# Sample states as the moving operand in a hybrid decoder step: four 32-column tiles, a predicated copy and two fold products

## What is computed

```python
def hgrn2_chunk(S, q, k, v, logf):
    b = jnp.cumsum(logf, axis=1)
    ...
    o = jnp.einsum('bhts,bshv->bthv', att, v) + jnp.einsum('bthk,bhkv->bthv', q * jnp.exp(b), S)
    b_last = b[:, -1]
    k_dec = k * jnp.exp(b_last[:, None] - b)
    S_new = jnp.exp(b_last)[..., None] * S + jnp.einsum('bshk,bshv->bhkv', k_dec, v)
    return S_new, o
```

## Time and profile before

| What | Value |
|---|---|
| Median of 3 runs | 1325.11 us (1325.05 to 1325.72) |
| The profiled execution, its own time | 1324.93 us |
| Its span, first to last instruction | 1323.0 us |
| TensorE, matmul / weight load busy | 1286.8 / 1224.3 us |
| VectorE / ScalarE / GpSimd busy | 585.6 / 519.6 / 261.1 us |
| Stage of the eight heads, within the span | about 61 to 550 us |

### The profile page before, as it was taken

How to read it: one execution, slowest core, us unless ns; L and a number is a source line. 1 busy time by engine, 2 the same in 40 slices (tenths; PEclk the granted TensorE clock), 3 DMA queues, 4 the chain that set the end, 5 groups by cost and what they waited for, 6 DMA issues and landing times.

```text
span 1323.0 us, 22284 instructions
## 1 busy us (share of the span) xinstructions
PE 1286.8 (97%) x8892; PEld 1224.3 (93%) x8892; DVE 585.6 (44%) x1213; ACT 519.6 (39%) x1035; POOL 261.1 (20%) x119
## 2 busy tenths in 40 slices
PE   4999999999999999999999999999999999999998
PEld 4999999999999999999999999999998899999885
DVE  5546657574847465600000155555555202335122
ACT  6453635445353535511111255555555314114111
POOL 0222221222322222222222111111110111342000
PEclk9999999999999999999999999999999899999999
DMA  6212121302021221121111311111100312241330
GB/s 197 66 33 66 35 64 34 79 18 79 18 79 34 78 56 43 34 64 48 48 41 43 84 33 33 33 33 33 33 17 1 106 32 64 58 102 33 116 126 37
DMA packets 136767, 73.85 MB, mean 56 GB/s; under 512 B 37185, under 2 KB 133138, under 8 KB 136690
## 3 DMA queue, kind: packets, MB, share of 16 engines
q1 hardware_dynamic: 136706, 72.99, 20.0%
HBM read 63.77 MB, written 10.22 MB: 56 GB/s over the span
## 4 chain that ended last, share of the span: by engine, by line
PE 62%; issue 25%; POOL 6%; DVE 4%; ACT 2%; DMA 1%; SPq 0%; POOLq 0%; ACTq 0%
PE pj L972 43%; POOL w_l L560 5%; PE pj L988 3%; PE pj L1319 3%; DVE scores L1595 2%; PE ps_a L1319 1%; PE ps_e L1319 1%; PE ps_e L1210 1%; PE ps_a L1175 1%; PE ps_d L1210 1%; DVE scores L1583 1%; PE ps_d L1319 1%; PE ps_b L1319 1%; PE ps_c L1319 1%; PE ps_a L1198 1%
## 5 line engine op out<-in xcount | busy, mean ns | idle before, releaser
L972 PE MATMUL pj<-xn_h,w_h 128*128 128x352 f32 x1704 | 563.2, 330 | 5.6 <-POOL w_l L560 2.1
L972 PE MATMUL pj<-xn_h,w_l 128*128 128x352 f32 x1704 | 551.5, 324 | 0.0
L972 PE MATMUL pj<-xn_l,w_h 128*128 128x352 f32 x1704 | 551.2, 323 | 0.0
L560 POOL TENSOR_TENSOR w_l<-w_raw,w_h 128x1024 fp32r<-128x1024 f32 x82 | 203.4, 2480 | 689.8 <-ACT w_h L632 689.8
L972 PEld LDWEIGHTS pj<-xn_h,w_h 128*128 128x128 f32 x1704 | 323.7, 190 | 15.1 <-issue 5.3
L972 PEld LDWEIGHTS pj<-xn_l,w_h 128*128 128x128 f32 x1704 | 324.4, 190 | 0.1
L972 PEld LDWEIGHTS pj<-xn_h,w_l 128*128 128x128 f32 x1704 | 323.8, 190 | 0.0
L632 ACT ACTIVATE w_h<-w_raw 128x1024 fp32r<-128x1024 f32 x82 | 86.4, 1054 | 114.4 <-PE pj L972 100.2
L1552 DVE TENSOR_TENSOR mg<-sg,pj 128x352 f32 (+1 forms) x24 | 12.4, 522 | 151.8 <-PE pj L972 150.4
L840 ACT ACTIVATE scores<-scores,stat 128x256 f32<-128x256 f32 (+1 forms) x128 | 61.4, 481 | 0.0
L972 PE MATMUL pj<-hl_l,w_h 128*128 128x352 f32 x168 | 54.2, 323 | 0.0
(11 more groups left out here) (361 smaller groups left out, 2014.4 us busy)
## 6 DMA issues: line engine op xcount, KB each, us to landing
w_raw<-in_w_in_dram SPq DMA_DIRECT2D x132, 256.0 KB, 3.4
x_t<-in_x_prompt_dram SPq DMA_DIRECT2D x8, 512.0 KB, 9.4
s<-in_state_hgrn_dram SPq DMA_DIRECT2D x8, 512.0 KB, 4.2
out_dram<-s SPq DMA_DIRECT2D x8, 512.0 KB, 3.2
w_raw<-in_w_pa_dram SPq DMA_DIRECT2D x16, 256.0 KB, 3.0
w_raw<-in_w_pb_dram SPq DMA_DIRECT2D x16, 256.0 KB, 4.3
wo_raw<-in_w_out_dram SPq DMA_DIRECT2D x8, 512.0 KB, 3.6
x_o<-in_x_prompt_dram SPq DMA_DIRECT2D x8, 512.0 KB, 4.1
```

Of the source, the lines that this page charges most:

```text
L560: g.tensor_tensor(w_l[p][:], w_raw[p][:], w_h[p][:].bitcast(F32), ALU.subtract).then_inc(w_lo_ready, 1)
L972: mm = nc.tensor.matmul(pj[g][:, 0:W], w[:, kt, :], x[:, kt, span(g)], start=(kt == 0 and m == 0), stop=(kt == KT - 1 and m == 2))
```

## The change

The sample part of `os` is taken apart. A new step `cr` on TensorE, behind `ps` and ahead of `u0`, takes the queries of all 32 sample tokens (`qI[:, SEQ:T]`, 128x32) as the stationary operand and streams each of the 8 states (128 columns) past them, into one of four groups of 32 partitions of `ps_e`, two states side by side. So every token's query meets every state. VectorE then copies, by a predicate `own`, only those rows in which token and state belong together, into an SBUF tile `cross` of 128x256 that is otherwise zero (step `crm`, ahead of `att0`). Last, `os` becomes three products of 32 moving columns: the one with `att_s` as before and two with the halves of `cross` as the stationary operand and a constant `fold` (128x32, a sum of identity columns) as the moving one. `fold`, the zeros in `cross` and `own` are made once ahead of the heads, `own` from four small loads. The wait for `s0` and the one for `qI` on TensorE move up to `cr`, and `s8` waits for `cr` in place of `ps`, since both lie in `ps_e`. GpSimd's program is the same.

```diff
-    masked = ["att0", "att1", "atts"]
+    masked = ["crm", "att0", "att1", "atts"]
...
+        cross = sb("cross", [P, 2, P])
+        fold = sb("fold", [P, NS])
+        own_b = sb("own_b", [P, NB])
+        own = sb("own", [P, 2])
...
+            for j in range(4):
+                sp.dma_start(own_b[j * NS:(j + 1) * NS, :], c_batch[0:NS, :]).then_inc(own_loaded, 16)
...
                 nc.tensor.matmul(ps_e[0:NS, 256:256 + NS], dk[:, SEQ:T], dq[:, SEQ:T], start=True, stop=True).then_inc(pe_done, pe.tick(now, "ps"))
+
+                t.wait_ge(s0_loaded, i * 16 + 16)
+                t.wait_ge(dve_done, dve.at(now, "qIm"))
+                for m in range(NB):
+                    j = m % 4
+                    mm = nc.tensor.matmul(ps_e[j * NS:(j + 1) * NS, m // 4 * P:(m // 4 + 1) * P], qI[:, SEQ:T], s0[:, m, :], start=True, stop=True)
+                mm.then_inc(pe_done, pe.tick(now, "cr"))
...
                 t.wait_ge(dve_done, dve.at(now, "atts"))
-                t.wait_ge(dve_done, dve.at(now, "qIm"))
...
-                t.wait_ge(s0_loaded, i * 16 + 16)
-                nc.tensor.matmul(ps_d[:, 0:NS], v_tok[0:NS, NC, :], att_s[:, :], start=True, stop=True)
-                for m in range(NB):
-                    e = SEQ + DEC * m
-                    mm = nc.tensor.matmul(ps_d[:, DEC * m:DEC * (m + 1)], s0[:, m, :], qI[:, e:e + DEC], start=False, stop=True, skip_group_check=True)
-                mm.then_inc(pe_done, pe.tick(now, "os"))
+                nc.tensor.matmul(ps_d[:, 0:NS], v_tok[0:NS, NC, :], att_s[:, :], start=True, stop=False)
+                nc.tensor.matmul(ps_d[:, 0:NS], cross[:, 0, :], fold[:], start=False, stop=False)
+                nc.tensor.matmul(ps_d[:, 0:NS], cross[:, 1, :], fold[:], start=False, stop=True).then_inc(pe_done, pe.tick(now, "os"))
...
+            v.tensor_reduce(fold[:], ident[:].rearrange("p (j t) -> p t j", j=4), mybir.AxisListType.X, ALU.add).then_inc(dve_done, dve.tick(pr, "fold"))
+            v.memset(cross[:], 0.0).then_inc(dve_done, dve.tick(pr, "cross0"))
+            v.wait_ge(own_loaded, 64)
+            for j in range(4):
+                rows_j = slice(j * NS, (j + 1) * NS)
+                v.tensor_copy(own[rows_j, :], own_b[rows_j, j::4]).then_inc(dve_done, dve.tick(pr, f"own{j}"))
...
-                        need(pe, pe_done, "ps")
+                        need(pe, pe_done, "cr")
...
+                v.copy_predicated(cross[:], own[:].bitcast(I32).rearrange("p (h o) -> p h o", o=1).to_broadcast([P, 2, P]),
+                                  ps_e[:, 0:2 * P].rearrange("p (h v) -> p h v", h=2)).then_inc(dve_done, done("crm"))
```

More of the change, by code:

```diff
@@ L144, in hybrid_step @@
         ("pro", ["par", "lbm", "lbd0", "lbd1", "lbs", "lbr", "lb", "oml", "noml", "mean"] + per_tile(["xn"], ["lo_a", "lo_b"])
-         + ["att0", "atts0", "reset", "reset_p", "reset_s"] + exponents[:2] + each_slot("q") + exponents[2:] + each_slot("z"), 1, 0),
+         + ["att0", "atts0", "reset", "reset_p", "reset_s", "fold", "cross0", "own0", "own1", "own2", "own3"] + exponents[:2] + each_slot("q") + exponents[2:] + each_slot("z"), 1, 0),
         ("head", ["ha"] + products + chain + masked + exponents + ["q0"] + gated_head
@@ L159, in hybrid_step @@
     ])
-    head_products = ["vt0", "vt1", "vts", "kt0", "kt1", "kts", "p0", "p1", "ps", "u0", "u1",
+    head_products = ["vt0", "vt1", "vts", "kt0", "kt1", "kts", "p0", "p1", "ps", "cr", "u0", "u1",
                      "o0", "o1", "os", "us0", "us1", "ms0", "ms1", "mss"]
@@ L343, in hybrid_step @@
         consts_loaded, g_loaded, masks_loaded, g_fin_loaded = sem("consts_loaded"), sem("g_loaded"), sem("masks_loaded"), sem("g_fin_loaded")
+        own_loaded = sem("own_loaded")
         s0_loaded, slopes_loaded, caches_loaded, bias_s_loaded = sem("s0_loaded"), sem("slopes_loaded"), sem("caches_loaded"), sem("bias_s_loaded")
```

## The result

Sixteen runs of the changed kernel have a median of 1329.43 us, sixteen of the kernel before, on the same chips, 1325.68 us. The ratio is 1.0027 with a 95% interval of 1.0020 to 1.0035: **slower by 2.7 to 4.6 us**, where 4 us were forecast. The profiled execution took 1329.47 us (span 1327.5).

What follows compares the result with a forecast made beforehand. TensorE, busy 97% of the span, was taken to bound the kernel. Heads 1, 2, 4, 6 add 4.1 us, heads 0, 3, 5 add 0.8, the last -0.9: +4.0, median 1329.0 us, range 1320 to 1334.

Steps and rivals of the forecast that it cites:

- The step that decides: GpSimd's `s0` scaling, freed 1.36 us earlier, collides with VectorE; head 2's square sums come 0.6 us later.
- `os`: On TensorE, 16 narrow passes (1.81 us) give way to two folds (0.45 us): done 1.36 us earlier after `u0`.
- `cr`: Sixteen added TensorE passes ahead of `u0`, overlapping in four column tiles: 0.43 us per head.
- The serial rival: `cr` runs pass by pass, 1.81 us in place of 0.43 in eight heads: 11 us more, 1340; 7%.
- The copy: Predicated VectorE copy ahead of `att0`: about 0.43 us, delaying what follows by about 0.36 us.
- Per head: 0.43 for `cr` plus 0.6 for later square sums: +1.03 us against an undisturbed head.
- the slow clock: TensorE's clock drop behind the narrow passes goes in heads 0, 3 and 5, giving back 0.77 us each.
- The rival of the late collision: L1437 gets through before GpSimd and only `sq_l` waits: +1.9 us, 1327.0 as a median; 17%.
- The last head: No exponents behind `att`, so square sums move forward: -0.9 us; its own slow clock hidden behind a wait.

Runs made afterwards that it cites:

- the releases: Changed kernel with GpSimd's scaling released by `cr`: 1308.64 us; its split for the next head held behind `sq_l`: 1321.53; scaling released by eighth product behind `os`: 1332.72.
- the second pair: Profiles from running both kernels once more, unchanged: changed kernel 1329.36 us, kernel before 1325.33 us.
- the first pair: First profiles of both kernels: profiled execution 1329.47 us for the changed kernel, 1324.93 us for the kernel before.

## Why the prediction was right

**The step that decides** held row for row. With the 3.10 us by which `u0` lies later now (221.87 against 218.77), the working for head 2 reads, forecast and measured: scaling from 235.84 (236.00) to 237.9 (237.90); the split's end 240.3 (240.26); L1453's end 240.9 (240.82); `q0` 240.85 (240.74); `sq_l` ready at 242.76 (242.65); the third GpSimd instruction from 241.2 (241.34), which holds it to 243.6 (243.74); `so1` done at 246.5 (246.63); square sums 246.55 (246.68). That these rows are the cause and not company is shown by the releases: moved GpSimd turns alone, with no work added or removed, take the kernel to 1308.6 or 1321.5 or 1332.7 us.

**`os`.** 1.36 us were forecast, 1.23 measured: the chunk outputs start 0.11 us later behind `u0` than before (9.64 against 9.53), and the two folds take 0.46 us (235.29 to 235.75), as taken.

**`cr`.** 0.43 forecast; from the first pass of `ps` to `u0` it was 0.18 us in head 2 and is 0.61: 0.43. The serial rival falls.

**The copy.** It takes 0.45 us; from its start to that of `att0` it is 0.33, near the 0.36 taken.

**Per head.** 1.03 forecast against an undisturbed head, 1.10 to 1.22 measured in heads 1, 2, 4 and 6. In heads 3 and 5 the slow clock is gone, as forecast (granted 1.00 behind `os` in all eight): +0.38 against +0.26. Heads 0 to 6 together: +4.9 forecast, +4.99 and +4.63 in the two pairs of profiles. In the second pair the kernel before has the slow clock in four of these heads, not three, for which the same working gives +4.1.

**Head 0 went between the forecast and a rival.** There the exponents stand 0.12 us earlier against `u0` (13.95 against 14.07 us for L1437 before the change), L1450 is through before the scaling takes its turn, and L1453 is held for that one turn only:

```profile
112.03 0.18 DVE L1450 SCALAR_TENSOR_TENSOR dk<-cs,b 128x32 f32<-128x32 f32 x1
112.25 2.32 DVE L1453 TENSOR_SCALAR dk<-dk 128x1056 f32<-128x1056 f32 x1
```

The head is 0.4 us shorter than before instead of 0.26 longer. The rival of the late collision, to which I gave 17%, has L1453 untouched and asks for a shift of 0.45 us; without the copy, 0.33 us brought it about. So the forecast for the other heads held by a narrow margin: 0.12 us changed the collision and 0.33 us replaced it by another.

**The last head.** -0.9 was forecast for its square sums. From `ps` to them it is 22.62 us before and 21.35 with the change in the first pair of profiles, 22.12 and 21.34 in the second: -1.27 and -0.78. The wait of 1.21 us in the earlier trace rows belongs to a head in which the clock fell behind `os`; at full clock it is 2.30 us before the change and 2.31 with it, so TensorE and VectorE did move together. Two things the forecast had wrong. It took the slow clock there as hidden, but `so0` on VectorE waited 0.41 us for TensorE's state updates:

```profile
546.84 0.69 DVE L1521 TENSOR_TENSOR s<-s,ps_a 128x512 f32<-128x512 f32 x1 [0.41 <-PE ps_a L1109]
```

And it has nothing on what comes behind the wait. From `u0` to the next projection by L979 (L972 before) it is 36.41 against 35.81 us in the first pair and 34.61 against 36.29 in the second: the clock fell behind the wait in one profile of each kernel.

**The total** of the first pair, +4.54 us, holds two items that are not the change's: the prologue's slow stretch (+1.8 us there) and the one at 1050 us (about -3); with the heads (+5.0) and the last head up to that projection (+1.0) they come to that sum. So the first pair owes its closeness partly to items that cancel. The second pair has both stretches on either side and differs by 4.03 us: +4.6 from the heads, -1.2 from the last head, in which the clock fell only before the change, and +0.8 from what lies ahead of the first `ps`, which comes between 95.2 and 97.2 us in the three profiles without the change; the rest gives -0.2. Counted from the first `ps` to the last head's square sums, which is the part that the forecast works out, the pairs give +3.7 and +3.9 us; +4.0 was forecast, and the medians of sixteen runs differ by 3.75.

## What to carry to other kernels

When a step is shortened on the bounding engine, look up who else waits for it: here its end released work on GpSimd, and that work, 1.2 us earlier, ran into VectorE rows that read SBUF alone. Read GpSimd and VectorE as one timeline, ask of each GpSimd instruction which VectorE rows around it work SBUF to SBUF, and put it beside rows that read PSUM. And after a change moves the last reader of a buffer, move the release as well: the wait that was right before (`os`) was almost 14 us too late afterwards, and cutting it turned 0.27% slower into 1.3% faster.

## What was not expected of the hardware

- A price of a small instruction that depends on the neighbour alone: in one and the same profile the 32 columns of L1450 took 0.18 us in head 0 and 1.90 in head 2, and 0.12 us in the place of the exponents against `u0` decided which.
- The clock fell behind a wait of 2.1 us in every second head of one kernel, behind one of 1.87 us in two of seven heads of another, and behind one of 2.31 us in one of two profiles of the changed kernel, although TensorE had been busy with full projections ahead of them. Behind the waits of 1.20 and 1.09 us of the changed kernel's heads it did not. Why one wait is followed by it and the next, of the same length, is not, these runs leave open.
